# A turned copy of x for layer 0, and 1/rms put behind layer 0's products

## The chip, the cores and the metric

One core of one Trainium2 chip runs the whole program. The metric is the device time of one execution in microseconds (us): 278.81 us, the median of 3 runs that lie between 278.06 and 280.2.

## The reference, cut to what matters

A trunk of two layers on x of 256 rows by 1024 columns, in float32.

```
def rms_norm(x, g):
    return x * rsqrt(mean(x * x, -1) + 1e-6) * g
hn = rms_norm(h, norm_g[0])                 # h = x at first
u, v, g_a, q, k, vv, g_b = split(hn @ w_in) # 1024 -> 7 * 512
y_a = gelu(u) * (tril(W_s) @ layer_norm(gelu(v)) + b_s) * silu(g_a)
y_b = causal_attention(q, k, vv) * silu(g_b)   # 8 heads of 64
h = h + concat(y_a, y_b) @ w_out
hn = rms_norm(h, norm_g[1])                 # layer 1: q, k, v, gate of 1024 columns each,
h = h + (dilated_attention(q, k, v) * silu(g)) @ w_out1
out = rms_norm(h, final_norm_g)
```

The division by the root mean square multiplies each row of hn by one number, so it can as well be applied to a row of the product hn @ w_in. Queries and keys are made turned (columns of the head on the partitions, the 256 rows of x along the free side), so there it is a factor per column.

## The kernel before, in words

**Weights.** Each product is made in float32 precision from two rounded parts: ScalarE (ACT) copies a quarter of a weight block to `w_hi` ("round", L529) and VectorE (DVE) subtracts it from the original to give `w_lo` ("rest", L670). The products are hi by hi, lo by hi and hi by lo (L896 to L898, or L882 to L886 for queries and keys). A block is 1024 by 512, loaded by SyncE's queue (SP) in two halves of 1 MB (`w_raw`, 3 slots, L409); a half is split in two quarters (`w_hi` and `w_lo`, 9 slots). A quarter is 2 chunks of 128 rows. SP's load of half n waits until the rests of half n-3 are done.

**Order.** `plan()` lists the halves, the groups of PSUM banks and the items. An item is the products of one quarter, in two steps, one for each chunk. In layer 0 the groups are: the attention's values (tile 0 of x's rows, then tile 1, each over both halves of the block), queries, keys, v, gate b, u, gate a, output. `steps()` then writes one list of steps, and each engine does its part of every step strictly in the order of this list. What lies outside of the products is put in by position (`at(...)`): twice the number of an item, plus 0 or 1 for its step. Rounds are put ahead of the first step of an item, as many as a credit allows: it grows by 2 with each whole item up to 5, and each round takes 1. A round waits for its half's load; ACT does nothing behind it until then.

**Start.** SP loads the first 128 rows of x, the gains, two half loads of the first weights, the other 128 rows, and so on. ACT and DVE take the sums of squares, GpSimd (POOL) makes the root (`root_of_squares`, L449 to L457), DVE scales the rows (L661, L679), PE turns them (`hidden_turn`, L821), and ACT and DVE split the turned rows with the gain into `hnT_hi` and `hnT_lo` (L504, L648). For tile 1 the same comes after tile 0's products have begun. Extra matmuls on the identity (L837) keep PE at work until then.

**Queries and keys.** When a group is done, ACT copies the banks' halves to the hi part (L539), DVE subtracts for the lo part (L702), and a second copy of the keys' hi part is made ("again", L386, half of it on ACT, half on DVE). The scores of head 0 and 1 stand three product steps behind the last product of the keys. The masks of layer 1 ("windows", L610 to L620) are made on DVE within the keys' group.

Of the kernel before, what the change touches and what calls it, by code (L numbers as in the profile page):

```python
# [20 lines left out]
P = 128  # L21
SEQ = 256
TILES = SEQ // P
D = 1024
# [33 lines left out]
    (8, ("gelu_inner", 4)), (9, ("gelu_outer", 4)), (10, ("layer_norm", 0)), (13, ("layer_norm", 1)),  # L58
    (20, ("mix", 0)), (26, ("mix", 1)), (24, ("gating", 0)), (29, ("y_pair", 0)), (29, ("y_pair", 1)),
    (25, ("gelu_inner", 6)), (27, ("gelu_outer", 6)), (27, ("mix_u", 0)), (30, ("mix_u", 1)),  # L60
# [3 lines left out]
    (-13, ("residual", 0, 0)), (-10, ("residual", 0, 1)), (-6, ("scale", 0)), (-3, ("hidden", 2)),  # L64
    (-2, ("residual", 1, 0)), (4, ("residual", 1, 1)), (5, ("scale", 1)), (12, ("hidden", 3)),
# [8 lines left out]
HIDDEN_1_AT, WINDOWS_AT, WS_AT = (5, 10, -2)  # L74
KEYS_AGAIN_AT = (5, 6, 5)
KEYS_AGAIN_BY = ("act", "dve")
WARM = (6, 4, 10)


def plan():  # L80
# [28 lines left out]
    groups.extend([("value_half", 0), ("value_half", 1)])  # L109
    halves.extend(("even_in", part * HALF_CHUNKS, vv) for part in range(2))  # L110
    for tile in range(TILES):
        items.extend((tile, i, q_, 0) for i in range(2) for q_ in range(2))
# [22 lines left out]
HALVES, GROUPS_OF_BANKS, ITEMS = plan()  # L135
LAST_ITEM_OF_GROUP = {item[0]: n for n, item in enumerate(ITEMS)}
LAST_ITEM_OF_QUARTER = {2 * item[1] + item[2]: n for n, item in enumerate(ITEMS)}
VALUE_KINDS = ("value_half", "value_tile")
# [3 lines left out]
def steps():  # L142
# [3 lines left out]
    out = [("round", 0), ("rest", 0), ("hidden", 0), ("round", 1), ("rest", 1), ("round", 2), ("rest", 2),  # L146
           ("squares", 1), ("round", 3), ("norm", 1), ("rest", 3)]
# [14 lines left out]
    at(HIDDEN_1_AT, ("hidden", 1))  # L162
    at(2 * first_item[2] + WINDOWS_AT, ("windows", 0))
    even = 2 * first_item[4]
    at(even + WS_AT, ("ws", 0))
# [3 lines left out]
    odd = 2 * first_item[10]  # L169
    for place, step in NORM_AT:  # L170
        at(odd + place, step)
    for last_keys, place in zip((3, 13, 15), KEYS_AGAIN_AT):
        at(2 * first_item[last_keys + 1] + place, ("again", last_keys, 1))
    heads(1, 2 * first_item[14])
    heads(2, 2 * first_item[16])
    for place, step in ODD_AT:
        at(2 * first_item[17] + place, step)
# [47 lines left out]
def build(nc, x, norm_g, final_norm_g, ab_w_in, ab_w_out, gmlp_ln_g, gmlp_ln_b, gmlp_w_s, gmlp_b_s,  # L225
# [12 lines left out]
    with ctx:  # L238
# [11 lines left out]
        hn = sb("hn", [P, TILES, D])  # L250
        hnT_hi = sb("hnT_hi", [P, CHUNKS, SEQ], fp32r)
# [20 lines left out]
        rstd = sb("rstd", [P, 8])  # L272
        power = sb("power", [P, 1])
        gain_rows = sb("gain_rows", [2 * CHUNKS, P])
# [5 lines left out]
        ws = tanh[:, 0, :].rearrange("p (b s) -> p b s", s=P)  # L280
# [23 lines left out]
        gains_loaded, gains_turned, gains_ready = sem("gains_loaded"), sem("gains_turned"), sem("gains_ready")  # L304
# [12 lines left out]
        ws_masked, ws_turned, wsT_ready = sem("ws_masked"), sem("ws_turned"), sem("wsT_ready")  # L317
        squares_dve = sem("squares_dve")
        squares, with_eps, rstd_ready = sem("squares"), sem("with_eps"), sem("rstd_ready")
        with_gain, final_act = sem("with_gain"), sem("final_act")  # L320
        first_scaled = sem("first_scaled")
        w_first = [sem(f"w_first{i}") for i in range(2)]
# [42 lines left out]

        def set_of_heads(group):

            return count_of_kind(SPLIT_KINDS, group - 1) // 2
# [24 lines left out]
        def _(sp):  # L393
            sp.dma_start(h[:, 0, :], x_tiles[0]).then_inc(x_loaded[0], 16)
            sp.dma_start(gain_rows[:], norm_g.rearrange("l (c p) -> (l c) p", p=P)).then_inc(gains_loaded, 16)
            for n, (matrix, chunk, column) in enumerate(HALVES):
# [5 lines left out]
                if n < 2:  # L402

                    sp.dma_start(w_raw[:, n, 0:2], rows[:, 0:2]).then_inc(w_first[n], 16)
                    if n == 1:
                        sp.dma_start(h[:, 1, :], x_tiles[1]).then_inc(x_loaded[1], 16)
                    sp.dma_start(w_raw[:, n, 2:4], rows[:, 2:4]).then_inc(w_loaded[n], 16)
                    continue
                sp.dma_start(w_raw[:, n % RAW_SLOTS], rows).then_inc(w_loaded[n % RAW_SLOTS], 16)  # L409
                if n == 2:  # L410

                    sp.wait_ge(squares, 3)
                    sp.dma_start(ws, gmlp_w_s[0].rearrange("g t s -> t g s")).then_inc(ws_loaded, 16)
                    sp.dma_start(ln_g, gmlp_ln_g.partition_broadcast(P)).then_inc(ln_loaded, 16)
                    sp.dma_start(ln_b, gmlp_ln_b.partition_broadcast(P)).then_inc(ln_loaded, 16)
                    sp.dma_start(bias_s[:], gmlp_b_s[0].rearrange("g t -> t g")).then_inc(bias_loaded, 16)
            for t in range(TILES):
                sp.wait_ge(scaled, 2 * (2 * TILES - 1) + t + 1)
# [6 lines left out]
        def _(pool):  # L425
            nc.gpsimd.memset(power[:], -0.5)
# [17 lines left out]
            def root_of_squares(n):  # L444

                first, second = sumsq[:, n, 0:1], sumsq[:, n, 1:2]

                pool.wait_ge(squares, 1 if n == 0 else 2 * n)
                nc.gpsimd.tensor_scalar(first, first, EPS, None, ALU.add).then_inc(with_eps, 1)  # L449
                if n == 0:  # L450
                    pool.wait_ge(squares_dve, 1)
                else:
                    pool.wait_ge(squares, 2 * n + 1)
                pool.wait_ge(with_eps, 2 * n + 1)
                nc.gpsimd.tensor_tensor(first, first, second, ALU.add).then_inc(with_eps, 1)
                pool.wait_ge(with_eps, 2 * n + 2)
                nc.gpsimd.tensor_tensor(rstd[:, n:n + 1], first, power[:], ALU.pow).then_inc(rstd_ready, 1)  # L457

            root_of_squares(0)
            root_of_squares(1)  # L460
# [538 lines left out]
```

## Time and profile before

| | |
|---|---|
| median of 3 runs | 278.81 us (278.06 to 280.2) |
| the profiled execution | 279.57 us, of it a span of 277.8 us from the first to the last instruction |
| PE busy | 266.2 us (96% of the span) |
| DVE busy | 182.2 us (66%) |
| ACT busy | 162.1 us (58%) |
| POOL busy | 16.6 us (6%) |
| DMA | 43.53 MB, mean 157 GB/s |
| mean granted TensorE clock | 0.988 |

PE is at work in nine tenths or more of each fortieth of the span but the first two, the third and the last. The chain that ended last is 88% PE, 5% DVE, 4% ACT and 1% POOL.

### The profile page before, as it was taken

The page shows a single profiled execution, that of the slowest core. Times are in us where ns is not written, and L with a number is a line of the kernel's source. Part 1 is how long each engine was busy: PE and PEld are TensorE (multiplying, and loading weights), DVE is VectorE, ACT ScalarE, POOL GpSimd, SP SyncE. Part 2 cuts the span into 40 slices and gives each one's busy share as a digit, 9 for nine tenths or more (in the row PEclk, how much of TensorE's full clock was granted, in tenths as well). Part 3 has the DMA queues.
Part 4 walks back from the last instruction along what each step waited for, and adds up shares of the span by engine and source line. Part 5 has one row for each costly group of instructions (what it writes and reads, how often), then busy time and mean ns, then how long its engine had stood idle before and what let it go on. Part 6 is the DMA issues. An engine that isn't in the chain of part 4 may idle for free.

```text
span 277.8 us, 4330 instructions
## 1 busy us (share of the span) xinstructions
PE 266.2 (96%) x1637; PEld 237.2 (85%) x1637; DVE 182.2 (66%) x341; ACT 162.1 (58%) x316; POOL 16.6 (6%) x38
## 2 busy tenths in 40 slices
PE   6979999999999999999999999999999999999990
PEld 6858999888888888888788999999999888888880
DVE  2886759895879397576777527494953958542643
ACT  3947685778484365256547637478676875650132
POOL 4140000100110000001100000000000001000021
PEclk9989999999999999999999999999999999999997
DMA  6986992654306634454554970828043323100004
GB/s 216 381 222 216 378 352 90 210 173 151 151 2 223 230 106 135 149 173 145 182 170 139 349 274 3 268 60 278 5 152 149 114 96 107 66 0 0 2 0 151
DMA packets 22499, 43.53 MB, mean 157 GB/s; under 512 B 1344, under 2 KB 1872, under 8 KB 22480
## 3 DMA queue, kind: packets, MB, share of 16 engines
q1 hardware_dynamic: 22336, 42.74, 46.0%
q0 software_dynamic: 144, 0.52, 0.6%
q8 instruction: 13, 0.21, 0.3%
q14 instruction: 6, 0.05, 0.0%
HBM read 42.22 MB, written 1.05 MB: 156 GB/s over the span
## 4 chain that ended last, share of the span: by engine, by line
PE 88%; DVE 5%; ACT 4%; POOL 1%; issue 1%; POOLq 0%; DVEq 0%
PE products L896 16%; PE products L898 16%; PE products L897 16%; PE products L886 7%; PE products L884 7%; PE products L882 7%; PE turned L821 4%; DVE k_low L702 2%; PE attended L837 2%; PE attended L940 2%; PE attended L939 2%; PE scores L916 2%; PE scores L915 2%; DVE w_lo L670 2%; PE attended L938 2%; PE attended L821 1%
## 5 line engine op out<-in xcount | busy, mean ns | idle before, releaser
L670 DVE TENSOR_TENSOR w_lo<-w_raw,w_hi 128x1024 fp32r<-128x1024 f32 x76 | 91.0, 1222 | 10.7 <-ACT w_hi L529 9.9
L529 ACT CAST w_hi<-w_raw 128x1024 fp32r<-128x1024 f32 x76 | 78.1, 1049 | 34.1 <-PE products L898 15.6
L896 PE MATMUL products<-w_hi,hnT_hi 128*128 128x512 f32 x144 | 58.4, 406 | 0.6 <-DVE w_lo L670 0.6
L897 PE MATMUL products<-w_hi,hnT_lo 128*128 128x512 f32 x144 | 56.9, 395 | 0.0
L898 PE MATMUL products<-w_lo,hnT_hi 128*128 128x512 f32 x144 | 56.9, 395 | 0.0
L882 PE MATMUL products<-hnT_hi,w_hi 128*128 128x256 f32 x192 | 54.6, 285 | 0.0
L886 PE MATMUL products<-hnT_hi,w_lo 128*128 128x256 f32 x192 | 54.3, 283 | 0.0
L884 PE MATMUL products<-hnT_lo,w_hi 128*128 128x256 f32 x192 | 54.3, 283 | 0.0
L884 PEld LDWEIGHTS products<-hnT_lo,w_hi 128*128 128x128 f32 x192 | 36.8, 192 | 0.1
L882 PEld LDWEIGHTS products<-hnT_hi,w_hi 128*128 128x128 f32 x192 | 36.7, 191 | 0.1
L886 PEld LDWEIGHTS products<-hnT_hi,w_lo 128*128 128x128 f32 x192 | 36.7, 191 | 0.0
L570 ACT ACTIVATE probs<-probs,least 128x128 f32<-128x128 f32 (+1 forms) x48 | 21.4, 447 | 20.2 <-DVE least L783 19.9
L898 PEld LDWEIGHTS products<-w_lo,hnT_hi 128*128 128x128 f32 x144 | 27.5, 191 | 6.1
L896 PEld LDWEIGHTS products<-w_hi,hnT_hi 128*128 128x128 f32 x144 | 27.5, 191 | 6.1 <-issue 1.3
L897 PEld LDWEIGHTS products<-w_hi,hnT_lo 128*128 128x128 f32 x144 | 27.5, 191 | 4.7
L896 PE MATMUL products<-w_hi,yT_hi 128*128 128x512 f32 x64 | 25.6, 400 | 0.0
L898 PE MATMUL products<-w_lo,yT_hi 128*128 128x512 f32 x64 | 25.0, 391 | 0.0
L897 PE MATMUL products<-w_hi,yT_lo 128*128 128x512 f32 x64 | 24.9, 390 | 0.0
L495 ACT ACTIVATE tanh<-h 128x512 f32<-128x512 f32 x11 | 7.0, 636 | 17.2 <-DVE h L808 15.3
L578 ACT COPY probsT<-turned 128x384 f32<-128x384 f32 x24 | 11.4, 476 | 6.9 <-PE turned L821 6.8
L898 PEld LDWEIGHTS products<-w_lo,yT_hi 128*128 128x128 f32 x64 | 12.0, 188 | 2.6
L897 PEld LDWEIGHTS products<-w_hi,yT_lo 128*128 128x128 f32 x64 | 12.0, 188 | 2.3
(124 smaller groups left out, 340.3 us busy)
## 6 DMA issues: line engine op xcount, KB each, us to landing
w_raw<-in_c_w_in SPq DMA_DIRECT2D x16, 1024.0 KB, 5.5
w_raw<-in_ab_w_in SPq DMA_DIRECT2D x12, 1024.0 KB, 5.6
w_raw<-in_ab_w_out SPq DMA_DIRECT2D x4, 1024.0 KB, 5.0
w_raw<-in_c_w_out SPq DMA_DIRECT2D x4, 1024.0 KB, 5.1
w_raw<-in_ab_w_in SPq DMA_DIRECT2D x4, 512.0 KB, 6.6
h<-in_x SPq DMA_DIRECT2D x2, 512.0 KB, 5.5
out<-hn SPq DMA_DIRECT2D x4, 256.0 KB, 2.2
gate<-in_final_norm_g POOLq DMA_DIRECT2D x1, 512.0 KB, 4.3
```

Of the source, the lines that this page charges most:

```text
L495: nc.scalar.activation(tanh[:, t, :], h[:, t, c * BLOCK:(c + 1) * BLOCK], ACT.Square, scale=D ** -0.5, accum_out=sumsq[:, n, c:c + 1]).the ...
L529: nc.scalar.copy(w_hi[:, n % SPLIT_SLOTS, :, :], w_raw[:, half % RAW_SLOTS, part, :]).then_inc(hi_ready, 1)
L570: last = nc.scalar.activation(probs[:, n % 2, a:b], probs[:, n % 2, a:b], ACT.Exp, scale=-1.0, bias=least[:, n, t:t + 1], accum_out=den[:, ...
L578: nc.scalar.copy(probsT[:, n % 2, :], turn_bank[:, 0:3 * P]).then_inc(probsT_ready, 1)
L670: nc.vector.tensor_tensor(w_lo[:, n % SPLIT_SLOTS, :, :], w_raw[:, half % RAW_SLOTS, part, :], w_hi[:, n % SPLIT_SLOTS, :, :].bitcast(fp32 ...
L821: return nc.tensor.matmul(to, of, ident[:], is_transpose=True, start=True, stop=True)
L882: nc.tensor.matmul(to, wh, hi[:, chunk, :], start=begins and c % 2 == 0, stop=False, skip_group_check=True)
L884: nc.tensor.matmul(to, wh, lo[:, chunk, :], start=False, stop=False, skip_group_check=True)
L886: last = nc.tensor.matmul(to, wl, hi[:, chunk, :], start=False, stop=ends, skip_group_check=True)
L896: nc.tensor.matmul(to[:], xh, w_hi[:, slot, half_item, :], start=begins, stop=False)
L897: nc.tensor.matmul(to[:], xl, w_hi[:, slot, half_item, :], start=False, stop=False)
L898: last = nc.tensor.matmul(to[:], xh, w_lo[:, slot, half_item, :], start=False, stop=ends)
```

## The change: what it does

- x comes in a second time, turned (`x_turned`, 128 by 8 chunks by 256). ACT and DVE split it with the gain straight into `hnT_hi` and `hnT_lo`, 8 chunks of 256 columns ("turned_x"). The scaling, the turning and the split of both tiles for layer 0 fall away, as do the gains' turn and the turn of gmlp_w_s (these come laid out as needed).
- The values' group takes both tiles of rows at once, quarter by quarter (4 items of 12 matmuls in place of 8 of 6), and its first chunk has hi, lo, and lo of the weight apart so that it can begin on one chunk.
- The sums of squares, now two ACT instructions of 1024 columns ("squares"), have position 5; SP loads x itself behind the third half of weights.
- POOL makes the roots of both tiles at once, half of them, and two diagonal matrices (`first_root`). PE multiplies ones by the diagonals ("rows", two float32 matmuls of 128 columns) and ACT copies the result to `rstd_rows`, 1/rms of each row on all partitions.
- The values' evacuation, the gates' and the gelus' activations take 1/rms as their scale. Queries and keys of layer 0 are multiplied by `rstd_rows` on DVE into `tanh` first (two more DVE instructions a group), and the hi and lo parts are made from there.

```diff
-HIDDEN_1_AT, WINDOWS_AT, WS_AT = (5, 10, -2)
+SQUARES_AT, ROWS_AT, WINDOWS_AT = (5, 2, 10)
...
-    out = [("round", 0), ("rest", 0), ("hidden", 0), ("round", 1), ("rest", 1), ("round", 2), ("rest", 2),
-           ("squares", 1), ("round", 3), ("norm", 1), ("rest", 3)]
+    out = []
+    for quarter in range(4):
+        out += [("turned_x", 2 * quarter), ("turned_x", 2 * quarter + 1), ("round", quarter), ("rest", quarter)]
...
+    at(SQUARES_AT, ("squares", 0))
+    at(2 * first_item[1] + ROWS_AT, ("rows", 0))
+    at(2 * first_item[1] + WINDOWS_AT, ("windows", 0))
...
-            while half == 0 and n >= 4 and split < 2 * len(HALVES):
+            while half == 0 and n >= 2 and split < 2 * len(HALVES):
...
+                if n == 0:
+                    sp.dma_start(w_raw[:, 0, 0], rows[:, 0]).then_inc(w_first[0], 16)
+                    sp.dma_start(w_raw[:, 0, 1], rows[:, 1]).then_inc(w_first[1], 16)
+                    sp.dma_start(xT[:, 2:4], x_turned[:, 2:4]).then_inc(xT_loaded[1], 16)
+                    sp.dma_start(w_raw[:, 0, 2:4], rows[:, 2:4]).then_inc(w_loaded[0], 16)
+                    sp.dma_start(xT[:, 4:8], x_turned[:, 4:8]).then_inc(xT_loaded[2], 16)
+                    continue
...
                 if n == 2:
+                    for t in range(TILES):
+                        sp.dma_start(h[:, t, :], x_tiles[t]).then_inc(x_loaded[t], 16)
+                if n == 3:
+                    sp.dma_start(wsT, gmlp_w_s[0]).then_inc(ws_loaded, 16)
                     sp.dma_start(ln_g, gmlp_ln_g.partition_broadcast(P)).then_inc(ln_loaded, 16)
                     sp.dma_start(ln_b, gmlp_ln_b.partition_broadcast(P)).then_inc(ln_loaded, 16)
...
+            def first_root():
+                pool.wait_ge(first_squares, TILES)
+                nc.gpsimd.tensor_scalar(mean_square[:], mean_square[:], EPS, None, ALU.add).then_inc(rstd_parts, 1)
...
+                nc.gpsimd.tensor_tensor(rstd[:, 0:TILES], mean_square[:], power[:].to_broadcast([P, TILES]),
+                                        ALU.pow).then_inc(rstd_parts, 1)
+                nc.gpsimd.tensor_scalar(ln_eps[:], mean_square[:], 4 * EPS, None, ALU.mult)
...
+                nc.gpsimd.tensor_scalar(half_rstd[:], rstd[:, 0:TILES], 0.5, None, ALU.mult).then_inc(first_rstd, 1)
+                for t in range(TILES):
+                    nc.gpsimd.tensor_scalar(diagonals[:, t, :], ident[:], rstd[:, t:t + 1], None,
+                                            ALU.mult).then_inc(diagonal_ready, 1)
...
+            nc.scalar.dma_start(xT[:, 0:2], x_turned[:, 0:2]).then_inc(xT_loaded[0], 16)
+            nc.scalar.dma_start(gain_of[:], norm_g).then_inc(gains_loaded, 16)
...
+                elif what == "squares":
+                    whole = tanh[:].rearrange("p t c -> p (t c)")
+                    for t in range(TILES):
+                        act.wait_ge(x_loaded[t], 16)
...
+                        nc.scalar.activation(whole, h[:, t, :], ACT.Square, scale=D ** -0.5,
+                                             accum_out=mean_square[:, t:t + 1]).then_inc(first_squares, 1)
...
+                    if heads_set == 0:
+                        dve.wait_ge(products_done, LAST_ITEM_OF_GROUP[n] + 1)
+                        dve.wait_ge(rows_ready, 1)
...
+                        for i, bank in enumerate(pair(n)):
+                            nc.vector.tensor_tensor(
+                                tanh[:, i, :].rearrange("p (a b) -> p a b", b=SEQ),
+                                bank[:].rearrange("p (a b) -> p a b", b=SEQ),
+                                rstd_rows[:].unsqueeze(1).to_broadcast([P, 2, SEQ]), ALU.mult).then_inc(heads_scaled, 1)
...
+                elif what == "rows":
+                    pe.wait_ge(diagonal_ready, TILES)
+                    for t in range(TILES):
+                        last = nc.tensor.matmul(turn_bank[:, t * P:(t + 1) * P], ones[:], diagonals[:, t, :],
+                                                start=True, stop=True)
+                    last.then_inc(rows_turned, 1)
```

## Rows read from the trace of the kernel before

**Rows 1.** Busy time by stretch: length, PE, PEld, DVE, ACT, POOL, clock, DMA share, GB/s.
```profile
5.00:10.00 5.00, 5.00 (x33) 4.96 (x33) 2.79 (x6) 3.07 (x10) 0.90 (x3) 1.00 1.04 394
...
16.00:18.00 2.00, 0.98 (x7) 0.74 (x8) 2.00 (x3) 0.40 (x2) 1.26 (x2) 1.00 0.92 160
...
20.00:22.00 2.00, 2.00 (x6) 1.57 (x6) 0.93 (x4) 0.00 (x0) 0.00 (x0) 0.58 1.05 409
```

**Rows 2.** The chain that ended last: start, length, engine, what is written, line.
```profile
2.11 2.93 PE attended L837 x12
...
14.93 2.70 DVE hn L679 x2
...
18.70 0.43 PE products L897
...
21.26 0.43 PE products L897
...
27.21 0.23 PE products L898
27.44 0.12 PE products L882
...
47.59 0.44 PE turned L821 x4
```

**Rows 3.** DMA issues of two short stretches: KB each, us to landing.
```profile
h<-in_x SPq DMA_DIRECT2D x1, 512.0 KB, 3.3
...
w_raw<-in_ab_w_in SPq DMA_DIRECT2D x1, 1024.0 KB, 10.4
```

**Rows 4.** SP's issues in order of time: start, length.
```profile
4.45 0.73 SPq L409 DMA_DIRECT2D w_raw<-in_ab_w_in  x1
...
14.01 0.51 SPq L414 DMA_DIRECT2D v<-in_gmlp_ln_g  x1
```

**Rows 5.** ACT in order of time: start, length, what; in brackets its wait.
```profile
26.81 2.00 ACT L529 CAST w_hi<-w_raw 128x1024 fp32r<-128x1024 f32 x2 [0.41 <-DMA w_raw<-in_ab_w_in]
...
50.95 2.38 ACT L539 CAST yT_lo<-products 64x512 fp32r<-64x512 f32 x4 [1.60 <-PE products L886]
53.23 1.25 ACT L386 CAST yT_lo<-yT_lo 64x512 fp32r<-64x512 f32 x2
```

**Rows 6.** Groups of instructions, 0 to 60 us: busy, mean ns, idle before.
```profile
L670 DVE TENSOR_TENSOR w_lo<-w_raw,w_hi 128x1024 fp32r<-128x1024 f32 x21 | 24.9, 1229 | 5.9 <-ACT w_hi L529 5.8
L529 ACT CAST w_hi<-w_raw 128x1024 fp32r<-128x1024 f32 x23 | 23.1, 1052 | 9.0 <-DMA w_raw<-in_ab_w_in 5.7 <-PE products L886 3.2
...
L504 ACT ACTIVATE hnT_hi<-scores,gain_of 128x128 fp32r<-128x128 f32 x8 | 2.2, 383 | 0.2 <-PE scores L821 0.2
L648 DVE SCALAR_TENSOR_TENSOR hnT_lo<-scores,gain_of,hnT_hi 128x128 fp32r<-128x128 f32 x8 | 2.2, 344 | 0.1
L495 ACT ACTIVATE tanh<-h 128x512 f32<-128x512 f32 x3 | 1.9, 649 | 1.9 <-DMA h<-in_x 1.8
...
L449 POOL TENSOR_SCALAR sumsq<-sumsq 128x1 f32<-128x1 f32 x2 | 1.1, 574 | 8.6 <-ACT tanh L495 8.6
L457 POOL TENSOR_TENSOR rstd<-sumsq,power 128x1 f32<-128x1 f32 x2 | 1.1, 570 | 0.2
...
L455 POOL TENSOR_TENSOR sumsq<-sumsq 128x1 f32<-128x1 f32 x2 | 0.4, 193 | 0.3 <-POOL sumsq L449 0.2
...
L430 POOL TENSOR_SCALAR_AFFINE_SELECT ident<-ident 128x128 f32<-128x128 f32 x1 | 0.3, 287 | 0.2 <-POOL mask_even L428 0.2
```

**Rows 7.** DVE in order of time, around the end of the keys' products.
```profile
48.88 2.56 DVE L670 TENSOR_TENSOR w_lo<-w_raw,w_hi 128x1024 fp32r<-128x1024 f32 x2
52.22 2.81 DVE L702 TENSOR_TENSOR k_low<-products,yT_lo 64x512 fp32r<-64x512 f32 x4 [0.78 <-ACT yT_lo L539]
```

**Rows 8.** PE in order of time: v's first product, head 0's first score.
```profile
50.74 0.40 PE L896 MATMUL products<-w_hi,hnT_hi 128*128 128x512 f32 x1
...
54.85 0.22 PE L915 MATMUL scores<-yT_lo,yT_hi 128*128 128x128 f32 x1
```

More of the change, by code:

```diff
@@ L107, in plan @@
     u, v, ga, q, k, vv, gb = (i * BLOCK for i in range(7))
[L109 to L112, printed above, removed]
+    whole("even_in", vv, "value", 0)
     whole("even_in", q, "query", 0)
@@ L425, in _ @@
         def _(pool):
+            nc.gpsimd.memset(ones[:], 1.0).then_inc(ones_ready, 1)
             nc.gpsimd.memset(power[:], -0.5)
@@ L541, in _ @@
                             last.then_inc(heads_high, 1)
-                    elif kind == "value_half":
-                        nc.scalar.mul(v[:, place, 0:BLOCK], pair(n)[0][:], 0.5).then_inc(act_emptied, 1)
+                    elif kind == "value":
+                        act.wait_ge(first_rstd, 1)
+                        for t, bank in enumerate(pair(n)):
+                            last = nc.scalar.mul(v[:, t, 0:BLOCK], bank[:], half_rstd[:, t:t + 1])
+                        last.then_inc(act_emptied, 1)
                     elif kind == "value_tile":
@@ L552, in _ @@
                         for t, bank in enumerate(pair(n)):
-                            nc.scalar.activation(tanh[:, t, :], bank[:], ACT.Tanh, scale=0.5).then_inc(tanh_ready, 1)
+                            half = half_rstd[:, t:t + 1] if n < FIRST_ODD else 0.5
+                            nc.scalar.activation(tanh[:, t, :], bank[:], ACT.Tanh, scale=half).then_inc(tanh_ready, 1)
                 elif what == "again" and KEYS_AGAIN_BY[step[2]] == "act":
@@ L892, in _ @@
                             targets = [(place, pair(group)[side])]
+                        if n == 0 and half_item == 0:
+                            pe.wait_ge(first_hi, 1)
+                            for wait, x_part, w_part in ((None, hi, w_hi), (None, lo, w_hi), (first_lo, hi, w_lo)):
+                                if wait is not None:
+                                    pe.wait_ge(wait, 1)
+                                for t, to in targets:
+                                    nc.tensor.matmul(to[:], x_part[:, 0, t * P:(t + 1) * P], w_part[:, 0, 0, :],
+                                                     start=wait is None and x_part is hi, stop=False)
+                            continue
                         for t, to in targets:
@@ L989 @@
     nc = bacc.Bacc("TRN2", target_bir_lowering=False, num_devices=1)
+    laid = {name: np.asarray(a) for name, a in inputs.items()}
+    laid["x_turned"] = laid["x"][0].T.reshape(CHUNKS, P, SEQ).transpose(1, 0, 2)
+    laid["norm_g"] = laid["norm_g"].reshape(2 * CHUNKS, P).T
+    laid["gmlp_w_s"] = laid["gmlp_w_s"].transpose(0, 3, 1, 2)
+    laid["gmlp_b_s"] = laid["gmlp_b_s"].transpose(0, 2, 1)
     arrays, args = {}, []
     for name in _NAMES:
-        a = np.ascontiguousarray(inputs[name])
+        a = np.ascontiguousarray(laid[name])
         arrays[f"in_{name}"] = a
```

271 lines of the change are left out of this document (139 added, 132 removed).

## The prediction

> **What bounds the kernel now.** I read the page's slices first: PE is full from the fourth slice on, so the time is the point at which PE begins to run without gaps plus the work behind it. The stretches [rows 1] show where it isn't full: PE is busy 0.98 us of the 2 us from 16, and behind that half-idle stretch the granted clock falls to half, the lower of its levels, 1.2 GHz (the stretch from 20 to 22 has a mean of 0.58). The chain of waits says why: DVE scales tile 1's rows until 17.6, then PE makes tile 1's products, at 0.43 us each while the clock is low and at 0.23 later, and the queries begin at 27.44 [rows 2]. From there on PE has no wait worth a tenth, so any later point of PE's list that is reached later by d costs d. The same holds for a gain: it counts only if no step further on has to wait for something else.
>
> **The first group.** The chunks of turned x cost ACT one instruction each (0.38 us for 128 columns [rows 6], half of the columns of one here; I take 0.45) and DVE one (0.34; I take 0.45). A quarter is then 0.9 + 1.05 = 1.95 us on ACT and 0.9 + 1.23 = 2.1 on DVE [rows 6], against 12 x 0.2275 = 2.7 us of PE (27.44 - 27.21 = 0.23 a product, [rows 2]). The first 512 KB land at 0.8 + 3.3 = 4.1 [rows 3] (weight chunk 0 and turned chunks 0 and 1 now), so the first product starts at about 5.8. The second quarter ends at 1536 KB. The missing 1.05 MB take 2.7 us at 394 GB/s [rows 1]; the queue of before fell 1.4 us behind that rate on its first 4096 KB (below), which I put all ahead of this: 8.2, and with round and rest ready at 8.2 + 1.05 + 1.23 = 10.5, say 10.6. Three quarters of products behind it: queries at 10.6 + 3 x 2.7 = 18.8, in place of 27.44. That is 8.6 us gained, if it stays. A low clock at the start (PE is idle from its extra matmuls to 5.8) is hidden by the wait for that second quarter.
>
> **Where it does not stay.** I worked the list of steps out by the rule in the code. Products of item 0 and 1 take no rounds now, the credit is 2, 4 and then its cap of 5 at item 2, so all of rounds 4 to 8 stand ahead of item 2's first step, and "squares" at position 5 stands behind them. Round 8 is the first of half 4 (the keys' first), so ACT reaches the squares only when half 4 has landed. PE's "rows" stands at position 10: ahead of the queries' second item, at 18.8 + 2.9 = 21.7. It needs the diagonals, these the root, this the squares. Everything of PE's list is queued behind that wait.
>
> When does half 4 land? Ahead of it in the queue: 2048 KB of values' weights, 1024 of turned x, half 2, x itself, half 3, 768 KB of gmlp weights and layer norm gains, and half 4, each of the unnamed ones 1024 KB. Before, 4096 KB up to the end of half 2 landed at 4.45 + 10.4 = 14.85 [rows 3, 4]; the same number of bytes lies there now. The other 3840 KB (3.93 MB) take 10.0 us at 394 GB/s [rows 1]: 24.8. But in the stretch from 16 to 18, when the two broadcast gains (issued from 14.01 [rows 4]) go through, the queues move 160 GB/s at a share of 0.92 [rows 1]: 0.52 MB at that rate are 3.3 us in place of 1.3. Part of that stretch is the small pieces of the bias, which are gone, so I take 1.5 of the 2.0: **half 4 at 26.3**, from 23.4 (3584 KB from 4.1 to 14.85 are 9.3 us at 394, so 1.4 were lost at the start; these made up, and no slow broadcast) to 27.5. The trace of before has it at 26.81 with less ahead of it but later issues [rows 5]. The Trainium skill (DMA: Bandwidth & Descriptors, Where 436 GB/s comes from) puts the ceiling of the 16 ports at 435 GB/s; an estimate by that page is 9.0 us for these bytes, half 4 at 23.9 and a total 2.4 us lower than mine. This case's best stretch shows 409 [rows 1]. The same page (Issuing engines are not separate DMA queues) says that the ACT-issued loads share the same 16 engines, which speaks against a gain by the second queue; no run here shows it.
>
> Round 8 is 1.05 us. A square of 1024 columns with its sum is bounded by 0.65 (the one of 512) and 2 x 0.65 [rows 6]; I take 1.2, so two are 2.4. POOL then has an addition (two of them took 1.15 us together, so with one at the 0.19 of its like the other took 0.95), the power 0.57, two small ones at 0.19 and two diagonals at 0.29 (nearest: the select on the same shape) [rows 6], with 0.1 between: 1.9 to 2.9 us. I take 2.0. The Trainium skill (SBUF — State Buffer, SBUF: two separate sides) says that a DVE instruction with two SBUF inputs, as a rest is, locks GpSimd's reads out for its whole length; by that rule rest 9, due just then, would cost up to 1.2 us more. One slow addition of two is all that this trace shows of it [rows 6]. So "rows" starts at 26.3 + 1.05 + 2.4 + 2.0 = **31.7**, 10 us after PE got there.
>
> Then: 0.5 us for the two matmuls (2.93 / 12 = 0.24 each, as the extra ones on the identity [rows 2]), three items of queries, 3/4 of (50.74 - 27.44) / 2 [rows 2, 8] = 8.7 us, and one stretch of low clock as the one seen after PE's wait of before: seven products at 0.43 in place of 0.23, and two partly, are 1.6 us more [rows 2]. Keys start at 42.5; before 27.44 + 11.65 = 39.1. **+3.4 us.** The gain of the first group is gone in the wait, all of it.
>
> **Other terms.** The turn of gmlp_w_s, 0.44 us of PE in the keys' group [rows 2], is gone: -0.4 to -0.5. The queries' evacuation gets two DVE instructions of 512 columns from PSUM (2.81 / 4 = 0.70 each, the nearest row [rows 7]); no one on PE waits for the queries yet, but DVE's work up to the keys' end, masks among it, gets 0.6 us later (1.4 for the two, 0.8 of it while ACT copies): it was done at 48.88 + 2.56 = 51.44 [rows 7], so now 1.3 us after the keys' last product. Only then come the keys' two multiplications; ACT's four copies (2.38) can begin after the first of them (0.7) and the second copy of the first bank (1.25) behind those [rows 5]. So it is there 1.3 + 0.7 + 2.4 + 1.25 = 5.65 us after the keys' products; the scores come at 54.85 - 50.74 = 4.1 [rows 8]. **+1.6 us**, from 0.2 (DVE free in time) to 2.5, and another 1.6 if the clock falls for it, which I leave to the upper end. The rests are safe: a rest stands six items ahead of its product. Gelu and gate activations only take another scale, the gating of the attention half another form of one instruction of the same length: 0. POOL's fill of `k_low` and its mask follow the root, at about 36, and are needed behind 50: 0. The first root's other consumer, the values' evacuation, must be done by the keys' start: ACT has 8 us for it, 0.
>
> Sum: 3.4 - 0.5 + 1.6 = +4.5 us. The profiled execution was 279.57 (277.8 of span, 1.8 around it), so 284.1 in it. It stood 0.8 above the median of 278.81: **283.3 us** for the median.
>
> **Rivals.**
> - *The same wait, but shorter.* Half 4 at 23.4, POOL in 1.6, no low clock and scores that wait 0.2: 4.5 - 2.9 - 0.4 - 1.6 - 1.4 = -1.8, 277.0 us. Between this and my sum the change ends within 1% of before, some 280 us. For it: the queue starts with two rings at work and fewer small pieces. Against: each of the four would have to go well, and the wait of before of less than 2 us did bring the low clock.
> - *No wait at rows: the gain stays.* The mechanism is ACT coming to the squares early. It decides if the diagonals are there when PE is, at 21.7, so the squares done by 19.7 and half 4 landed by 16.2. Then 18.8 - 27.44 = -8.6, -0.5, +1.6: 271.3 us. Against it: 8.13 MB by 16.2 is 502 GB/s even if bytes moved from 0 on, and no stretch shows more than 409 [rows 1]. What is left for it is a misreading of the list.
> - *The change does not do what it says*: the first group isn't shorter, for want of turned x. Its end may move from 18.8 to 28.8 without any effect, since "rows" must wait to 31.7 anyway; beyond that it adds. This is why I don't price the first group finer.
>
> **How the numbers follow.** The wait as computed 0.60, the shorter one 0.25, the gain that stays 0.15. About 1%, 2.8 us, is what a measurement of this kernel can tell from no change. Faster by more: 0.15; within: 0.25; slower: 0.60. Lower end 276.5, just under the best sum of the short wait (277.0). Upper: half 4 at 27.5 (+1.2), POOL +0.9, scores +0.9 and a second low clock +1.6 give 287.9; 288.5. Left out is mainly the case that the gain stays.
>
> **What would show it.** PE's first product near 6 and queries near 19; then one long idle stretch of PE, from about 22 to 32, ended by POOL's diagonals, ahead of the two float32 matmuls; ACT idle on the load ahead of round 8 and the squares right behind that; a granted clock of half behind it; the keys' first product at 42 to 43. A second wait of PE ahead of head 0's scores, ended by ACT's second copy of the keys. From there to the end it is as long as before. I am wrong if PE passes "rows" without a wait, if the squares run ahead of round 8, or if half 4 lands before 22.

## The result, and the profile after

The changed kernel takes 287.62 us (286.99 to 287.8, 4 runs) against 278.73, so the medians differ by 8.9 us. The ratio over all executions is 1.0296, with a 95% interval of 1.0265 to 1.0328. The profiled execution has a span of 285.8 us, 8.0 more than before. The forecast was 283.3 us, in a range of 276.5 to 288.5, slower.

First the stretches of the start, with the columns of [rows 1]: PE's busy time stands second, the granted clock after POOL's.

```profile
5.00:10.00 5.00, 1.50 (x4) 1.25 (x5) 2.43 (x6) 3.06 (x7) 0.00 (x0) 0.74 1.05 399
10.00:12.00 2.00, 2.00 (x6) 1.59 (x5) 1.82 (x4) 2.00 (x4) 0.00 (x0) 0.50 1.06 388
...
25.00:30.00 5.00, 0.25 (x3) 0.04 (x1) 1.35 (x2) 4.33 (x7) 0.92 (x2) 0.79 0.96 354
30.00:35.00 5.00, 1.45 (x7) 1.45 (x7) 2.60 (x3) 3.39 (x5) 5.00 (x8) 0.50 0.55 178
35.00:40.00 5.00, 5.00 (x32) 5.00 (x32) 3.58 (x3) 2.49 (x4) 1.37 (x2) 0.68 0.70 225
```

PE stops at 25.25 and is idle for the next 8.3 us. POOL, nearly idle in the whole kernel, is busy for all of 30 to 35. PE's waits, longest first (us in total, times, longest), name what ended them:

```profile
PE turned L1047 <- POOL hn L492: 8.3, 1, 8.3
PE products L967 <- DVE hnT_lo L734: 4.0, 1, 4.0
PE scores L992 <- ACT yT_lo L403: 2.2, 1, 2.2
```

L1047 is the row product, L492 the diagonals. The other two are the start of the first product and the scores of head 0. Before, there was no wait of PE behind 27.44 but 0.4 us at the turns of probabilities. ACT and POOL in order of time show what the first wait hangs on:

```profile
20.77 2.00 ACT L582 CAST w_hi<-w_raw 128x1024 fp32r<-128x1024 f32 x2 [3.29 <-DMA w_raw<-in_ab_w_in]
25.58 1.04 ACT L582 CAST w_hi<-w_raw 128x1024 fp32r<-128x1024 f32 x1 [2.81 <-DMA w_raw<-in_ab_w_in]
26.53 1.05 ACT L561 ACTIVATE tanh<-h 128x1024 f32<-128x1024 f32 x1
...
28.73 0.19 ACT L561 ACTIVATION_READ_ACCUMULATOR tanh<-h 128x1 f32 x1
```

```profile
29.00 0.24 POOL L484 TENSOR_SCALAR mean_square<-mean_square 128x2 f32<-128x2 f32 x1 [25.75 <-ACT tanh L561]
29.32 0.73 POOL L486 TENSOR_TENSOR rstd<-mean_square,power 128x2 f32<-128x2 f32 x1
30.02 1.18 POOL L488 TENSOR_SCALAR ln_eps<-mean_square 128x2 f32<-128x2 f32 x1
31.16 1.15 POOL L490 TENSOR_SCALAR half_rstd<-rstd 128x2 f32<-128x2 f32 x1
32.29 1.21 POOL L492 TENSOR_SCALAR hn<-ident,rstd 128x128 f32<-128x128 f32 x2
```

Round 8 waits until 25.58 for half 4, the squares come right behind it, and POOL passes the root on only at 33.5. On PE the wait, the keys' end and the scores stand thus (columns as in [rows 8]; the products of v begin where the keys' end):

```profile
22.21 0.28 PE L948 MATMUL products<-hnT_hi,w_hi 128*128 128x256 f32 x1
...
33.55 1.23 PE L1047 MATMUL turned<-hn,ones 128*128 128x128 f32 x4 [8.30 <-POOL hn L492]
...
56.30 0.40 PE L973 MATMUL products<-w_hi,hnT_hi 128*128 128x512 f32 x1
...
62.80 0.30 PE L992 MATMUL scores<-yT_lo,yT_hi 128*128 128x128 f32 x1 [2.23 <-ACT yT_lo L403]
```

The queries begin 27.28 - 22.21 = 5.1 us earlier (27.28 is where this view of before has what the chain of [rows 2] puts at 27.44), against [rows 8] v's products 56.30 - 50.74 = 5.6 later and the first score 62.80 - 54.85 = 7.95 later. From the first score to the end it is 223.0 us after and 222.95 before. So the whole loss is in the first 63 us.

DVE just ahead of the scores, to be read beside [rows 7]:

```profile
55.33 0.42 DVE L680 TENSOR_TENSOR mask_odd<-mask_odd,gate 128x256 f32<-128x256 f32 x1
55.67 2.55 DVE L729 TENSOR_TENSOR w_lo<-w_raw,w_hi 128x1024 fp32r<-128x1024 f32 x2
58.15 1.27 DVE L752 TENSOR_TENSOR tanh<-products,rstd_rows 128x512 f32<-128x512 f32 x2
```

The keys' multiplication (L752) comes 1.85 us after their last product, behind the masks and two rests.

### The profile page after: what moved, and what is told of

It is laid out like the page before. It is cut to its first block, busy times and chain, and to the rows that moved or that the text cites. A ratio compares the mean times of both kernels' runs of the same rounds, so it can differ in the third digit from the quotient of the medians.

```text
span 285.8 us, 4236 instructions
## 1 busy us (share of the span) xinstructions
PE 263.3 (92%) x1596; PEld 234.6 (82%) x1596; DVE 180.4 (63%) x332; ACT 162.7 (57%) x306; POOL 18.7 (7%) x41
## 4 chain that ended last, share of the span: by engine, by line
PE 74%; DVE 10%; ACT 5%; DMA 5%; issue 2%; POOL 2%; POOLq 0%; ACTq 0%; DVEq 0%
PE products L973 14%; PE products L975 14%; PE products L974 14%; PE products L948 6%; PE products L950 6%; PE products L952 6%; DVE w_lo L729 4%; PE turned L896 3%; DMA w_raw<-in_ab_w_in 3%; DMA gain_of<-in_norm_g 2%; DVE k_low L771 2%; PE attended L1017 2%; PE attended L1016 2%; PE scores L992 2%; PE scores L993 2%
## 5 line engine op out<-in xcount | busy, mean ns | idle before, releaser
L582 ACT CAST w_hi<-w_raw 128x1024 fp32r<-128x1024 f32 x75 | 77.3, 1047 | 38.8 <-PE products L975 15.4
L973 PE MATMUL products<-w_hi,hnT_hi 128*128 128x512 f32 x142 | 57.5, 405 | 0.0
L975 PE MATMUL products<-w_lo,hnT_hi 128*128 128x512 f32 x142 | 56.0, 394 | 0.0
L974 PE MATMUL products<-w_hi,hnT_lo 128*128 128x512 f32 x142 | 56.0, 394 | 0.0
L948 PE MATMUL products<-hnT_hi,w_hi 128*128 128x256 f32 x192 | 55.5, 289 | 0.0
L950 PE MATMUL products<-hnT_lo,w_hi 128*128 128x256 f32 x192 | 55.1, 287 | 0.0
L950 PEld LDWEIGHTS products<-hnT_lo,w_hi 128*128 128x128 f32 x192 | 37.6, 196 | 0.1
L948 PEld LDWEIGHTS products<-hnT_hi,w_hi 128*128 128x128 f32 x192 | 37.6, 196 | 0.1
L952 PEld LDWEIGHTS products<-hnT_hi,w_lo 128*128 128x128 f32 x192 | 37.5, 195 | 0.0
L632 ACT ACTIVATE probs<-probs,least 128x128 f32<-128x128 f32 (+1 forms) x48 | 21.4, 447 | 19.2 <-DVE least L858 18.9
L973 PE MATMUL products<-w_hi,yT_hi 128*128 128x512 f32 x64 | 25.6, 400 | 0.0
L640 ACT COPY probsT<-turned 128x384 f32<-128x384 f32 x24 | 11.4, 475 | 6.8 <-PE turned L896 6.8
L973 PEld LDWEIGHTS products<-w_hi,yT_hi 128*128 128x128 f32 x64 | 12.0, 188 | 2.3
```

Of the source, the lines that this page charges most:

```text
L582: nc.scalar.copy(w_hi[:, n % SPLIT_SLOTS, :, :], w_raw[:, half % RAW_SLOTS, part, :]).then_inc(hi_ready, 1)
L632: last = nc.scalar.activation(probs[:, n % 2, a:b], probs[:, n % 2, a:b], ACT.Exp, scale=-1.0, bias=least[:, n, t:t + 1], accum_out=den[:, ...
L640: nc.scalar.copy(probsT[:, n % 2, :], turn_bank[:, 0:3 * P]).then_inc(probsT_ready, 1)
L948: nc.tensor.matmul(to, wh, hi[:, chunk, :], start=begins and c % 2 == 0, stop=False, skip_group_check=True)
L950: nc.tensor.matmul(to, wh, lo[:, chunk, :], start=False, stop=False, skip_group_check=True)
L952: last = nc.tensor.matmul(to, wl, hi[:, chunk, :], start=False, stop=ends, skip_group_check=True)
```

## The experiments

The waits are PE's, and "keys x" is the start of the keys' multiplication on DVE, all in the profiled execution. All ratios are to the kernel before, whose medians beside these runs were 278.77 to 279.59. Most profiled executions lie within 1.1 us of their kernel's median; those of diagonals first (289.82) and scores later (277.54) were over 2 us above it.

| kernel | queries begin | wait at rows | keys x | wait at scores | median us |
|---|---|---|---|---|---|
| before | 27.28 | none | none | 0 | 278.73 |
| changed | 22.21 | 8.3 | 58.15 | 2.2 | 287.62 |
| rows late | 21.10 | 2.3 | 51.98 | 5.2 | 283.37 |
| masks early | 20.81 | 9.7 | 56.70 | 0.6 | 285.84 |
| diagonals first | 21.02 | 9.2 | 58.41 | 2.2 | 287.62 |
| squares early | 20.69 | 0 | 48.83 | 5.0 | 281.25 |
| both early | 22.04 | 0 | 48.73 | 3.6 | 280.25 |
| both, 17 matmuls | 20.19 | 0 | 48.52 | 4.7 | 280.40 |
| both, gains first | 21.19 | 0 | 48.45 | 4.2 | 280.57 |
| squares early, heads unscaled | 21.94 | 0 | none | 1.2 | 276.14 |
| squares early, masks first | 21.68 | 0 | 45.42 | 0.7 | 275.14 |
| the same, front shortened | 20.86 | 0 | 44.92 | 0.9 | 275.49 |
| the same, scores later | 21.48 | 0 | 46.00 | 0 | 275.40 |

**Rows late.**

```diff
-SQUARES_AT, ROWS_AT, WINDOWS_AT = (5, 2, 10)
+SQUARES_AT, ROWS_AT, WINDOWS_AT = (5, 7, 10)
```

> Position of PE's two row matmuls 2 -> 7 (seven product steps into the queries instead of two); nothing else. Theory W (PE stands in order behind a wait for POOL's diagonals, 8.3 us at 25.1 in the changed kernel): PE reaches the place at 22.2 + 7 x 1.46 = 32.4, the diagonals are there at 33.5 as before, the wait is about 1.1 us, no long low clock behind it, and the keys' products begin near 35.4 in place of 44.7: about 278.5 us, 9 us less. Rival D (the first half of the queries' and keys' time is set by supply of split weights, the wait only hides it): PE waits as long in other places and the time stays above 285.

283.37 us, 1.0167 (1.0124 to 1.021); 4.2 us less than the changed kernel, not 9. The wait at the rows did go, but another grew:

```profile
PE scores L992 <- ACT yT_lo L403: 5.2, 1, 5.2
...
PE turned L1047 <- POOL hn L492: 2.3, 1, 2.3
```

The first wait costs what theory W says: 6.0 us less of it, the low clock behind it gone, and v's products begin 9.2 us earlier (47.11). But 3.0 us came back ahead of the scores, and with a low clock from 56.6 to 60.0 the time from the first score to the end grew by 1.6 us. Supply of weights (rival D) didn't hold PE: no wait of a product behind the first.

**Masks early.**

```diff
-SQUARES_AT, ROWS_AT, WINDOWS_AT = (5, 2, 10)
+SQUARES_AT, ROWS_AT, WINDOWS_AT = (5, 2, 4)
```

> Only the masks of layer 1 (eleven DVE instructions, 3.5 us) are put six product steps earlier, position 10 -> 4, where DVE is idle. Theory S (the wait of 2.2 us ahead of head 0's scores is DVE coming late to the keys' multiplications, since the masks and two rests stand ahead of them): DVE multiplies the keys right at their end, the scores wait 0.2 to 0.5 us, and the time falls by 1.9 us to 285.7. Rival (the chain multiply, copy, copy again is too long by itself, wherever DVE is): the wait stays above 1.5 us and the time within 0.7 us of 287.6.

285.84 us, 1.0252 (1.0213 to 1.0292), 1.8 less, and the wait at the scores is 0.6. DVE now waits for the keys:

```profile
56.70 1.29 DVE L752 TENSOR_TENSOR tanh<-products,rstd_rows 128x512 f32<-128x512 f32 x2 [1.99 <-PE products L952]
```

Theory S holds for the changed kernel: the second wait is the multiplication queued behind the masks.

**Diagonals first.**

```diff
-                nc.gpsimd.tensor_scalar(ln_eps[:], mean_square[:], 4 * EPS, None, ALU.mult)
                 pool.wait_ge(rstd_parts, 2)
-                nc.gpsimd.tensor_scalar(half_rstd[:], ...).then_inc(first_rstd, 1)
                 for t in range(TILES):
                     nc.gpsimd.tensor_scalar(diagonals[:, t, :], ident[:], rstd[:, t:t + 1], ...
+                nc.gpsimd.tensor_scalar(half_rstd[:], ...).then_inc(first_rstd, 1)
+                nc.gpsimd.tensor_scalar(ln_eps[:], mean_square[:], 4 * EPS, None, ALU.mult)
```

> POOL makes the two diagonals right behind the power; the half and the multiple for the layer norm come after them. Theory L (POOL's instructions of 1.15 us are 0.2 to 0.3 us of work that stands until the end of a DVE rest with both inputs in SBUF): the two instructions behind the power, whichever they are, end with the two rests, the diagonals are there about 1.2 us earlier (32.3) and the rows begin there; 0.6 to 1.2 us less, as the clock is low behind the wait in any case. Rival (these instructions cost 1.15 us each on POOL by themselves): two fewer of them ahead, 2.3 us earlier. Other rival (only the diagonals are long): no change.

287.62 us, 1.0299 (1.0255 to 1.0342): no change. POOL in order of time:

```profile
30.09 3.10 POOL L490 TENSOR_SCALAR hn<-ident,rstd 128x128 f32<-128x128 f32 x2
33.15 0.23 POOL L492 TENSOR_SCALAR half_rstd<-rstd 128x2 f32<-128x2 f32 x1
33.34 0.23 POOL L493 TENSOR_SCALAR ln_eps<-mean_square 128x2 f32<-128x2 f32 x1
```

The small instructions of 1.15 us take 0.23 now, and the diagonals, which took 1.21 together, take 3.10: 2.51 for the first, which starts at 30.09, and 0.61 for the second. So neither kind is slow: what stands beside DVE's rests is, whichever it is. The time is what the other rival named, but its reason (only the diagonals are long) is not so. I had the gain wrong, since I did not count that the diagonals' own work (0.6 us each) isn't done under the rests either: the rests end at 32.2 in both orders and the work behind them is about the same. Whether it is the two inputs of a rest that do it, this run can't tell; the masks-first run below bears on it.

**Squares early.** SP loads x itself right behind the values' weights, ahead of half 2.

```diff
-SQUARES_AT, ROWS_AT, WINDOWS_AT = (5, 2, 10)
+SQUARES_AT, ROWS_AT, WINDOWS_AT = (3, 2, 10)
...
                     sp.dma_start(w_raw[:, 1, 2:4], rows[:, 2:4]).then_inc(w_loaded[1], 16)
+                    for t in range(TILES):
+                        sp.dma_start(h[:, t, :], x_tiles[t]).then_inc(x_loaded[t], 16)
                     continue
...
-                if n == 2:
-                    for t in range(TILES):
-                        sp.dma_start(h[:, t, :], x_tiles[t]).then_inc(x_loaded[t], 16)
```

> x itself is loaded ahead of the third half of weights, and the squares have position 3, so that ACT does them ahead of rounds 4 to 8; the rows stay at position 2. Theory W: ACT has the squares done by about 17.5, POOL the diagonals by 20 (no rest beside them), PE passes the rows without a wait and keeps its clock; the keys' products begin near 34.3, 10.3 us earlier, and with the scores' wait as it is the time is about 277.3. Rival D (supply): the later third half (18.0 in place of 15.4) delays the queries by 2 us or more, and the keys wait for their weights; time 280 or more.

281.25 us, 1.0073 (1.0045 to 1.0101). PE has no wait at the rows at all, and v's products begin at 44.16, 12.1 us earlier than in the changed kernel, somewhat more than theory W says. The queries weren't late, so rival D fell. Part is lost again further on: the scores wait 5.0 us instead of 2.2, and from the first score (53.48) to the end it is 225.7 us instead of 223.0. POOL in order of time, where DVE idles to 18.86 and has rests from 18.86 to 21.2:

```profile
17.35 0.26 POOL L487 TENSOR_SCALAR ln_eps<-mean_square 128x2 f32<-128x2 f32 x1
17.56 0.22 POOL L489 TENSOR_SCALAR half_rstd<-rstd 128x2 f32<-128x2 f32 x1
17.75 1.22 POOL L491 TENSOR_SCALAR hn<-ident,rstd 128x128 f32<-128x128 f32 x2
18.93 1.23 POOL L493 TENSOR_SCALAR gelu_rstd<-rstd 128x2 f32<-128x2 f32 x1
20.13 1.14 POOL L495 TENSOR_TENSOR quarter_rstd<-half_rstd 128x2 f32<-128x2 f32 x1
```

The same small instructions are 0.22 to 0.26 us alone and 1.14 to 1.23, the length of a rest, beside one. The Trainium skill (SBUF — State Buffer, SBUF: two separate sides) says that a DVE instruction with two SBUF inputs and a GpSimd instruction that reads SBUF share a pair of ports, and that the one which starts first holds it for its whole length. The trace agrees: each of these small instructions ends with the rest beside it.

**Both early** (squares early, and masks at 4).

```diff
-SQUARES_AT, ROWS_AT, WINDOWS_AT = (3, 2, 10)
+SQUARES_AT, ROWS_AT, WINDOWS_AT = (3, 2, 4)
```

> The kernel with the squares early (281.25 us; no wait at the rows, but 5.0 us ahead of head 0's scores and 6.8 us of low clock around it), and the masks at position 4 as well. Theory S (the scores wait since DVE reaches the keys 4.5 us after their last product, 3.5 of it the masks): the wait falls to 1.0 us or less, the low clock behind it goes, and 5 to 7 us are won: 274.5 to 276.5. Rival (DVE's delay comes from its start into the queries' multiplication behind a row of rests, and masks moved ahead of them only push that one later): DVE's work ends as late, the wait stays at 3 us or more, 279 or more.

280.25 us, 1.0028 (1.0002 to 1.0054); the wait at the scores is 3.6. Theory S in its first form fell, the rival held: the keys' multiplication starts at 48.73 against 48.83. The wait is shorter only because PE came later: the queries began 1.35 us later, the first score 0.1 earlier (53.38). DVE in order of time:

```profile
38.16 1.22 DVE L728 TENSOR_TENSOR w_lo<-w_raw,w_hi 128x1024 fp32r<-128x1024 f32 x1
39.29 1.28 DVE L751 TENSOR_TENSOR tanh<-products,rstd_rows 128x512 f32<-128x512 f32 x2
41.35 2.80 DVE L770 TENSOR_TENSOR yT_hi<-tanh,yT_hi 64x512 fp32r<-64x512 f32 x4 [0.78 <-ACT yT_hi L593]
44.18 4.63 DVE L728 TENSOR_TENSOR w_lo<-w_raw,w_hi 128x1024 fp32r<-128x1024 f32 x4
48.73 1.28 DVE L751 TENSOR_TENSOR tanh<-products,rstd_rows 128x512 f32<-128x512 f32 x2
```

Without the wait at the rows DVE is busy without a gap worth the name from 32.4 on, where the late halves of weights have landed, and masks moved within that stretch move nothing behind it. This gave a new form (S2): from 32 on DVE's list has a fixed length, whatever PE does, and only work put into its idle time before 32 helps.

**Both early, 17 extra matmuls** and **both early, gains first.**

```diff
-WARM = 8
+WARM = 17
```

> As with both early, and 17 extra matmuls at the start in place of 8, to the first product at 8.5 us. Theory C (the idle time from 4.5 to 8.5 brings a low clock from 8 to 11.4 or 14.3 us, and the first group is held by it): full clock from the start, queries begin about 1 to 2 us earlier, total 1 to 1.5 us below the one with both early. Rival (the first group is held by the splits of the second and third quarter): clock full, start of the queries within 0.4 us, no difference.

```diff
+            nc.scalar.dma_start(gain_of[:], norm_g).then_inc(gains_loaded, 16)
             nc.scalar.dma_start(xT[:, 0:2], x_turned[:, 0:2]).then_inc(xT_loaded[0], 16)
-            nc.scalar.dma_start(gain_of[:], norm_g).then_inc(gains_loaded, 16)
```

> As with both early, and ACT issues the load of the gains (8 KB in pieces of 64 B) ahead of the first two chunks of turned x. Theory G (the gains, 5.7 us from issue to landing, hold ACT's first split until 6.9): it starts when the turned chunks land, near 6.2, and the queries 0.5 to 0.8 us earlier. Rival (small loads land with the large ones around them): no change beyond 0.3 us.

280.40 us, 1.0029 (1.0006 to 1.0052), and 280.57, 1.0051 (1.0022 to 1.008). The queries begin 1.85 and 0.85 us earlier, and the time is what it was: the wait at the scores is 4.7 and 4.2 instead of 3.6. Both totals were foretold too low, by S's first form; they are what S2 asks for, since the keys are multiplied at 48.5 in each.

How much of the earlier queries is C's and G's is less plain. The eight kernels of the table that start alike (8 extra matmuls, turned x first) begin their queries anywhere from 20.69 to 22.21, by how long the clock stays low at the start. C holds for the clock: with 17 extra matmuls the products are 0.23 us apart from the first on, and the queries begin 0.5 us earlier than the earliest of the eight. G holds for the load: issued first, the same 8 KB land after 3.0 us instead of 5.3, ACT's first split starts at 6.15 instead of 6.59 and the first product at 7.70 instead of 8.14. That is 0.44 us; the rest of the 0.85 lies within that spread.

**Squares early, heads unscaled.** Masks at 10. Queries and keys of layer 0 are not multiplied by 1/rms: ACT and DVE read the banks, the two added DVE instructions and their waits are out.

```diff
-            return (tanh[:, 0, :], tanh[:, 1, :]) if set_of_heads(group) == 0 else pair(group)
+            return pair(group)
...
-                        for i, bank in enumerate(pair(n)):
-                            nc.vector.tensor_tensor(
-                                tanh[:, i, :].rearrange("p (a b) -> p a b", b=SEQ), ...
...
```

> The kernel with the squares early, masks at 10 again, but queries and keys of layer 0 are left without their factor 1/rms: no multiplication on DVE, ACT copies straight from the banks as in the kernel before (a part of the computation is left out). Theory S: it is the added multiplication standing on DVE behind the masks and rests that makes the scores wait; ACT now copies at the keys' end, the wait falls from 5.0 to about 0.6 us, no low clock, about 274 us. Rival (the queue of rests after the earlier rows is late by itself): the wait stays above 3 us.

276.14 us, 0.9874 (0.9825 to 0.9922), 5.1 less than with the multiplication. The wait is 1.2 and it is DVE's lo part, not ACT's copy, that ends it:

```profile
PE scores L976 <- DVE k_low L755: 1.2, 1, 1.2
```

So the multiplication is what makes DVE's place matter: 2.6 us of work on DVE, and, more, ACT's copies that must now stand behind DVE. The time was 2 us over what was expected. 0.6 of it is this wait, and 1.25 is the start: the queries began at 21.94, against 20.69 with the squares early, in the spread described above.

**Squares early, masks first.**

```diff
-SQUARES_AT, ROWS_AT, WINDOWS_AT = (3, 2, 10)
+SQUARES_AT, ROWS_AT, WINDOWS_AT = (3, 2, -8)
```

> Squares early, and the masks ahead of item 0's step in the list, where DVE sat idle from 15.4 to 18.9 us (it waits for the load of half 2 there). Theory S2 (the scores wait for DVE's work in its order; its busy stretch begins at about 32 us, when the late halves have landed, whatever PE does; only work taken out of that stretch helps): 3.5 us less of DVE between 32 and 49, keys multiplied right at their end near 45.9, scores wait 0.5 to 1 us, no low clock: 275.5 to 276.5 us, under the kernel before. Rival (the multiply-copy-copy chain itself is the wait): 3 us or more of wait and 279 or more.

275.14 us, 0.9861 (0.9829 to 0.9893): faster than both kernels, with the whole computation. The masks run from 15.48 to 19.2 on DVE while it waits for half 2, the keys' multiplication starts 3.4 us earlier, and PE's waits are

```profile
PE products L966 <- DVE hnT_lo L733: 3.5, 1, 3.5
...
PE scores L991 <- issue: 0.7, 1, 0.7
```

S2 holds. The time is 6.1 us less than with the squares early alone. In the profiled executions the first score comes 3.4 us earlier (50.09 against 53.48; PE waits 4.3 less, but the queries began 1.0 later), and from there to the end it is 2.7 us less (223.0 against 225.7). The second part fits the low clock. The stretch from 50 to 60, first with the squares early, then with the masks first:

```profile
50.00:60.00 10.00, 6.52 (x21) 5.54 (x22) 9.00 (x19) 8.09 (x17) 0.00 (x0) 0.66 0.59 193
```

```profile
50.00:60.00 10.00, 9.90 (x51) 8.48 (x52) 8.73 (x20) 8.17 (x19) 0.00 (x0) 1.00 0.52 163
```

The granted clock is 0.66 in the mean behind the wait of 5.0 us, and full behind 0.7.

This run also bears on POOL's slow instructions. Here `half_rstd` runs beside a mask instruction of DVE with one tensor input, and takes what it takes alone:

```profile
17.66 0.29 DVE L676 TENSOR_SCALAR gate<-gate 128x256 f32<-128x256 f32 x1
17.80 0.22 POOL L489 TENSOR_SCALAR half_rstd<-rstd 128x2 f32<-128x2 f32 x1
```

The same is seen with the front shortened (18.21, 0.22 us). So not every instruction of DVE holds POOL. That the second SBUF input of a rest is what does fits both, but no run here changes that input alone.

**The same, front shortened** (gains first, 15 extra matmuls) and, on top, **scores later.**

```diff
-WARM = 8
+WARM = 15
...
-     (3, 3, 6, 9, 10, 12, 13, 17)),
+     (5, 5, 6, 9, 10, 12, 13, 17)),
```

The second change is the later kernel's alone.

> As with the masks first, and the gains' load first on ACT's queue and 15 extra matmuls, so that the queries begin near 20 in place of 22. Theory S2: the keys then end at 44 but DVE's stretch is where it was, so the scores wait 1.5 to 2.5 us more: total within 0.7 us of the one with the masks first. Rival (PE sets the time now): 1.5 to 2 us less.

> As the last one, and the scores of heads 0 and 1 two product steps later (2.7 us), so that PE has products to do where it would wait. Theory S2: the wait ahead of the scores falls by up to 2.7 us and, if the softmax chain behind them has slack, the time by as much, to 274; if it has none, PE waits ahead of the first turn of probabilities instead and the time stays.

275.49 us, 0.9894 (0.9854 to 0.9934), and 275.40, 0.988 (0.9843 to 0.9918): the same as without, within what these runs tell. In the first the total fell where S2 puts it, but not by the mechanism stated: the queries begin at 20.86, only 0.8 us earlier, and the scores wait 0.2 us more, not 1.5 to 2.5. PE is held earlier instead: by the split of the values' second quarter (0.7 us, at 11.4) and by that of quarter 4 at the queries' start (1.0). In the second the first turn of probabilities waits (1.8) in place of the scores. So neither the splits of the first quarters nor the softmax chain leave room here.

**The kernel before, masks moved** (position 10 to -9, DVE's idle time from 20.9).

> The kernel before, with its masks put ahead of the last product step of item 3, where its DVE idles from 20.9 us; nothing of the change. If the win of the version with the masks first (275.14 us) is the change's, this one stays within 1 us of 278.8: PE has no wait behind 27.44 that DVE's delay could cause. Rival (the place of the masks is the win by itself): 276 or less.

279.24 us, 1.0001 (0.9976 to 1.0025). Without the change the masks' place is worth nothing that these runs could tell (0.25%, 0.7 us).

## Why the prediction was right, and where it was too small

**The first group.** Queries were expected at 18.8 and began at 22.21. Two terms: the gains, 8 KB issued second on ACT's queue, took 5.7 us from issue to landing and held ACT's first split to 6.94, so the first product came at 8.50 and not at 5.8; and the clock was at half from 7.4 to 14.3, behind PE's idle time from 4.5. I had called that hidden by the wait for the second quarter. It was not: PE had no such wait, and 8.50, 48 products at 0.2275 (10.9) and 2.8 for the low clock make the 22.2. As the prediction argued, all this cost nothing: the wait at the rows stood behind it (10 us forecast, 8.3 measured, since PE came 3.4 us later and the diagonals 1.85).

**The wait at rows.** Its mechanism was as stated, step by step: half 4 at 25.6 (26.3 forecast), the squares done at 28.92 (29.75), both inside their bounds. The step that was mis-sized is the term "POOL 2.0 us": it took 4.5, and the rows began at 33.55 and not at 31.7. Of the 2.5 us, 1.9 are the two small instructions at 1.15 beside rests 9 and 10, and 0.6 the diagonals at 0.6 each, for which the select of the same shape (0.29 [rows 6]) was no measure. The rule of the Trainium skill that DVE's two inputs lock GpSimd out (SBUF — State Buffer, SBUF: two separate sides) was weighed in the prediction as one rest of 1.2 us and left out of the sum; two rests stood there and two instructions met them.

**The low clock behind it.** 1.6 us forecast, 2.3 measured: half clock from 33.55, where PE resumed, to 38.15 is 4.6 us, not 3.4. With the rows 1.85 later this makes 2.55 of the 2.7 us by which v's products are later than forecast (5.6 against 3.4 - 0.5).

**The scores.** +1.6 us forecast, +2.4 measured (62.80 - 56.30 = 6.50 against 4.11). The chain was right: DVE behind masks and rests, multiply, copy four times, copy again. DVE was 1.85 us behind the keys' end, not 1.3; the other 0.3 is in the steps behind it.

**The rest of the kernel** is unchanged to 0.1 us, as said. 1.85 + 0.7 + 0.8 are 3.35 of the 3.5 us between the sum, +4.5, and the +8.0 of the spans. The medians differ by 8.9; the profiled execution of before stood 0.8 above its median, which the forecast had allowed for.

**The range.** That 287.62 lies within it, 0.9 us below the upper end, is in part luck. The upper end had 1.2 us for a late half 4, and it came 0.7 early; it had 0.9 for POOL, and 2.5 were needed.

**The rivals.** The shorter wait did not happen; each of its four terms went the other way but half 4's landing. That the gain stays happened only when ACT was let come to the squares early, which is the mechanism the prediction gave for it; its price, 271.3, was too good, for it had neither the 22 us of the first group nor DVE's stretch from 32 on. That the first group's end could move freely was seen up to 22.2: in masks early it came 1.4 us earlier (20.81), PE waited 1.4 longer at the rows, and they began at 33.49, against 33.55 in the changed kernel. Later than that was not tried. Where the wait at the rows was gone, moving it by up to 1.85 us also moved nothing, since DVE's place held the scores.

What stays open: how much of each kernel's time is the length of its low stretches of clock. In the profiled executions with 8 extra matmuls the products of the start are 0.43 us apart until a point between 11.4 and 14.3, though eight of these kernels start alike and PE is idle 3.4 to 4.0 us in each of the eight. Nor does the same wait always bring a low clock: in the kernel before, the granted clock was 0.57 from 18 to 20 behind PE's wait of 1.8 us; in the one with the masks moved, behind the same wait, it was 1.00 from 16 to 24, and the queries began at 25.21. No run here isolates what decides it.

The clock column has to be read with care at the start. With the masks first it says 1.00 from 8 to 12 (the column after POOL's), and PE's products in the same stretch stand 0.43 us apart, the spacing of the low clock:

```profile
8.00:12.00 4.00, 3.67 (x9) 2.93 (x10) 3.83 (x7) 3.96 (x8) 0.00 (x0) 1.00 1.04 400
```

```profile
11.03 0.63 PE L972 MATMUL products<-w_hi,hnT_hi 128*128 128x512 f32 x1
11.45 0.63 PE L973 MATMUL products<-w_hi,hnT_lo 128*128 128x512 f32 x1
```

From 13.5 on they are 0.23 apart. The same holds with both early and the gains first (to 13.0) and with the heads unscaled (to 13.4). Near the start the spacing of equal products tells the clock; that column alone does not.

## What to carry to other kernels

When the work ahead of a step is shortened, look in each engine's own list for what now stands ahead of the next producer: here five splits, the last bound to a load, stood before two instructions that a short PE step needed, and 5 us won turned into 8 us waited. A wait removed brings the next one: after the rows it was DVE's queue ahead of the scores, and only work put into DVE's idle time before the loads landed, not just earlier within its busy stretch, moved it. A move of an independent piece that is worth nothing before a change can be what makes the change pay.

## What the hardware showed that I had not expected

- A POOL instruction on 128 by 2 elements took 0.22 to 0.26 us alone and 1.14 to 1.23 beside DVE's 1.23 us subtraction of two SBUF operands; two in a row met two subtractions, each in full. One diagonal of 0.61 us took 2.51 beside two of them.
- DVE can be the one that is held, and I overlooked this in the kernel before. Its two scalings of a tile's rows take 0.88 us for tile 0 and 2.69 for tile 1, where POOL fills `k_low` and masks a tile beside them. They end at 17.6, and PE's wait of 1.8 us hangs on them. That POOL is the cause is a reading of these rows; moving the fill, which might have won part of what the change was made for, was not tried.

```profile
6.17 0.88 DVE L661 TENSOR_SCALAR hn<-h,rstd 128x512 f32<-128x512 f32 x2 [1.37 <-POOL rstd L457]
...
14.77 1.80 POOL L462 MEMSET k_low<- 128x2048 f32 x1
14.93 2.69 DVE L679 TENSOR_SCALAR hn<-h,rstd 128x512 f32<-128x512 f32 x2 [1.18 <-POOL rstd L457]
```

- 8 KB in 64-byte pieces, issued second on ACT's queue behind 256 KB, landed 5.3 to 5.7 us later; issued first, they landed after 3.0 (both early with the gains first). Small pieces alone did not make this load slow, then; nor did being second: in the kernel before the same 8 KB in 512-byte pieces, issued behind 512 KB, took 3.0.
- Half 4, with 7936 KB in all, could be used at 25.58. The queues ran at a share of 0.96 to 1.06 and 354 to 410 GB/s in every stretch from 5 to 30 us; no stretch was as slow as the 160 GB/s of [rows 1], which I had put down to the broadcast gains.
